# First block's input and first two weight pieces made one stage earlier, in the projection outputs' memory

## What is computed

```python
def rmsnorm(x, g):
    y = xf * lax.rsqrt(jnp.mean(xf * xf, axis=-1, keepdims=True) + NORM_EPS)
    return (y * g.astype(jnp.float32)).astype(x.dtype)

def swiglu(x, w_in, w_out):
    gate, up = jnp.split(x @ w_in, 2, axis=-1)
    return (jax.nn.silu(gate) * up) @ w_out

def decoder_layer(x, ...):
    x = x + 0.5 * swiglu(rmsnorm(x, lp['norm_ffn1']), lp['ffn1_w_in'], lp['ffn1_w_out'])
    h = rmsnorm(x, lp['norm_mix'])
    proj = h @ lp['w_in']
    ...
    x = x + jnp.concatenate([y_rwkv, y_sc, y_ssm], axis=-1) @ lp['w_out']
    x = x + 0.5 * swiglu(rmsnorm(x, lp['norm_ffn2']), lp['ffn2_w_in'], lp['ffn2_w_out'])
```

## Time and profile before

| | |
|---|---|
| median of 3 runs | 1755.36 us |
| the profiled execution's own time | 1752.43 us |
| its span in the profile | 1750.6 us |
| TensorE matmul busy | 1592.8 us, 91% of the span |
| VectorE / ScalarE / GpSimd busy | 58% / 48% / 35% |
| granted TensorE clock, mean | 0.966 |
| DMA | 256 MB, 146 GB/s over the span |

### The profile page before, as it was taken

The page is one execution under the profiler, slowest core; times in us unless marked ns, Lnnn a source line. Parts: engine busy times, 40 slices in busy tenths (PEclk is TensorE's granted clock), DMA queues, the critical chain, the costliest instruction groups (busy, mean ns, idle before and its releaser), DMA issues. The chain is left out here.

```text
span 1750.6 us, 41466 instructions
## 1 busy us (share of the span) xinstructions
PE 1592.8 (91%) x17389; PEld 1507.6 (86%) x17389; DVE 1010.7 (58%) x1704; ACT 843.0 (48%) x1480; POOL 618.0 (35%) x407
## 2 busy tenths in 40 slices
PE   5999999988789899999789999997987999899996
PEld 4999999886678789999789999997766888899995
DVE  3543377685689776343354434968667887554433
ACT  2545464656244555444344444665553445554431
POOL 0434412322075533434233343132204653334340
PEclk9999999989899999999999999999989999999997
DMA  5555557452054544555354555645403454455550
GB/s 171 172 167 184 158 157 207 149 152 72 3 143 130 148 148 158 185 193 175 114 161 162 193 175 167 194 148 174 124 1 85 127 175 116 142 174 187 178 166 25
DMA packets 280490, 256.28 MB, mean 146 GB/s; under 512 B 48022, under 2 KB 268540, under 8 KB 280290
## 3 DMA queue, kind: packets, MB, share of 16 engines
q1 hardware_dynamic: 276538, 252.05, 46.2%
q10 hardware_dynamic: 3768, 1.59, 0.4%
HBM read 242.22 MB, written 11.38 MB: 145 GB/s over the span
## 5 line engine op out<-in xcount | busy, mean ns | idle before, releaser
L223 PE MATMUL ps<-front_h_hi,front_hi 128*128 128x264 f32 x1520 | 451.4, 297 | 35.4 <-DVE front_lo L210 31.4
L210 POOL TENSOR_TENSOR front_lo<-front_raw,front_hi 128x1024 fp32r<-128x1024 f32 (+1 forms) x104 | 256.8, 2469 | 546.3 <-ACT front_hi L203 546.3
L224 PE MATMUL ps<-front_h_lo,front_hi 128*128 128x264 f32 x1520 | 439.3, 289 | 0.0
L225 PE MATMUL ps<-front_h_hi,front_lo 128*128 128x264 f32 x1520 | 438.8, 289 | 0.0
L203 ACT ACTIVATE front_hi<-front_raw 128x1024 fp32r<-128x1024 f32 (+2 forms) x238 | 246.7, 1039 | 287.5 <-PE ps L225 250.1
L223 PEld LDWEIGHTS ps<-front_h_hi,front_hi 128*128 128x128 f32 x1520 | 294.5, 194 | 43.5 <-issue 39.4
L210 POOL TENSOR_TENSOR out_lo<-out_raw,out_hi 128x1024 fp32r<-128x1024 f32 (+1 forms) x84 | 198.7, 2367 | 312.0 <-ACT out_hi L203 312.0
L224 PEld LDWEIGHTS ps<-front_h_lo,front_hi 128*128 128x128 f32 x1520 | 294.5, 194 | 1.3
L225 PEld LDWEIGHTS ps<-front_h_hi,front_lo 128*128 128x128 f32 x1520 | 292.6, 193 | 0.1
L203 ACT ACTIVATE out_hi<-out_raw 128x1024 fp32r<-128x1024 f32 (+1 forms) x168 | 173.2, 1038 | 222.1 <-PE ps L225 182.2
L210 DVE TENSOR_TENSOR front_lo<-front_raw,front_hi 128x1024 fp32r<-128x1024 f32 (+1 forms) x134 | 163.0, 1217 | 119.2 <-ACT front_hi L203 119.2
(11 more groups left out here) (375 smaller groups left out, 3373.2 us busy)
## 6 DMA issues: line engine op xcount, KB each, us to landing
front_raw<-in_w_in SPq DMA_DIRECT2D x50, 1024.0 KB, 5.2
front_raw<-in_ffn_w_in SPq DMA_DIRECT2D x44, 1024.0 KB, 6.0
out_raw<-in_ffn_w_in SPq DMA_DIRECT2D x44, 1024.0 KB, 5.4
back_sample_rows<-row_scratch SPq DMA_DIRECT2D x160, 128.0 KB, 3.0
out_raw<-in_w_out SPq DMA_DIRECT2D x16, 1024.0 KB, 5.2
front_raw<-in_ffn_w_out SPq DMA_DIRECT2D x16, 896.0 KB, 4.6
out_raw<-in_ffn_w_out SPq DMA_DIRECT2D x16, 896.0 KB, 4.6
front_raw<-in_ffn_w_out SPq DMA_DIRECT2D x8, 1024.0 KB, 4.9
```

Of the source, the lines that this page charges most:

```text
L210: eng.tensor_tensor(self.lo[n % self.RING][:, 0:k, 0:w], self._raw(n), self.hi[n % self.RING][:, 0:k, 0:w].bitcast(F32), ALU.subtract).the ...
L223: pe.matmul(out, hi[:, j, 0:w], x_hi[:, j], start=start and j == 0, stop=False)
L224: pe.matmul(out, hi[:, j, 0:w], x_lo[:, j], start=False, stop=False)
L225: mm = pe.matmul(out, lo[:, j, 0:w], x_hi[:, j], start=False, stop=stop and j == k - 1)
```

## The change

- `load_stage` also loads pieces 0 and 1 of layer 0's ffn1 (2 MB, behind the five other loads on SyncE's queue) and SyncE waits for them before the stage ends; the gains are copied out before x instead of after it; ScalarE and VectorE make h hi and h lo of layer 0, VectorE two tiles behind its copies.
- `back_stage` of layer 0 does the same for layer 1: the two loads stand behind all its own pieces, and h hi and h lo are made as `following` of ffn2. Layer 1's back stage has nothing following.
- `front_stage` no longer makes h, no longer waits for it (`h_made=True`) and reads pieces 0 and 1 where they lie (`resident`). Its three raw buffers begin with pieces 2, 3 and 4. `split_lo(1)` stands before the fold, and the mean behind product 1 instead of product 2.
- `xs` and `ys` are allocated once for the program; h hi, h lo and the two pieces lie over them.

```diff
 class Stream:
@@ load
-        if p >= self.raw_ring:
+        if p >= self.raw_ring + len(self.resident):
             n = max(self.last[q] for q in range(p - self.raw_ring + 1)) + 1
             sp.wait_ge(self.hi_ready, n)
...
@@ split_hi
-        act.wait_ge(self.loaded[p % self.raw_ring], self.landed[p])
+        if p >= len(self.resident):
+            act.wait_ge(self.loaded[(p - len(self.resident)) % self.raw_ring], self.landed[p])
...
+class NextInput:
+    def act_hi(self, act, k):
+        act.wait_ge(self.x_ready, k + 1)
+        act.activation(self.env.in_hi[:, k], self.env.x[:, k], ACT.Copy, scale=self.gain(k)).then_inc(self.hi_done, 1)
+
+    def dve_lo(self, dve, k):
+        dve.wait_ge(self.hi_done, k + 1)
+        dve.scalar_tensor_tensor(out=self.env.in_lo[:, k], in0=self.env.x[:, k], scalar=self.gain(k), in1=self.env.in_hi[:, k].bitcast(F32),
+                                 op0=ALU.mult, op1=ALU.subtract).then_inc(self.lo_done, 1)
+
+    def sp_weights(self, sp, w_in):
+        wi = w_in[self.layer].rearrange("(k p) c -> p k c", p=P)
+        for part in range(2):
+            sp.dma_start(self.env.first_raw[part][:], wi[:, :, part * FF:part * FF + 2 * P]).then_inc(self.weights_in, 16)
+        sp.wait_ge(self.weights_in, 32)
...
@@ load_stage
+                first.sp_weights(sp, d["ffn1_w_in"])
...
                 for k in range(KT):
+                    if k == KT - 1:
+                        pe.wait_ge(gains_copied, 1)
...
+            @block.scalar
+            def _(act):
+                act.wait_ge(gains_copied, 1)
+                for k in range(KT):
+                    first.act_hi(act, k)
+
             @block.vector
             def _(dve):
-                for k in range(KT):
-                    dve.wait_ge(turned, k + 1)
-                    dve.tensor_copy(env.x[:, k], env.ps[:, k, 0:N]).then_inc(copied, 1)
                 dve.wait_ge(gains_turned, 1)
-                dve.tensor_copy(env.gains[:], env.ps[:, KT - 1, N:N + (DEPTH + 1) * KT]).then_inc(copied, 1)
+                dve.tensor_copy(env.gains[:], env.ps[:, KT - 1, N:N + (DEPTH + 1) * KT]).then_inc(gains_copied, 1)
+                for k in range(KT + 2):
+                    if k < KT:
+                        dve.wait_ge(turned, k + 1)
+                        dve.tensor_copy(env.x[:, k], env.ps[:, k, 0:N]).then_inc(copied, 1)
+                    if k >= 2:
...
+                        first.dve_lo(dve, k - 2)
@@ front_stage
-        ffn = Ffn(st, env, "ffn1", ws, 0, norm1, at, None, following=norm2, side=vec, mean_after=2)
+        ffn = Ffn(st, env, "ffn1", ws, 0, norm1, at, None, following=norm2, side=vec, mean_after=1, h_made=True)
...
-                for p in range(3):
+                for p in range(2, 5):
                     ws.load(sp, p)
                 vec.sp(sp)
                 more = Part(side(sp))
-                for p in range(3, len(pieces)):
+                for p in range(5, len(pieces)):
...
-                for k1 in range(KT):
-                    norm1.act_hi(act, k1)
                 ws.split_hi(act, 0)
...
-                for k1 in range(KT):
-                    norm1.dve_lo(dve, k1)
                 ws.split_lo(dve, 0)
+                ws.split_lo(dve, 1)
                 norm1.dve_fold(dve)
-                ws.split_lo(dve, 1)
                 ws.split_lo(dve, 3)
@@ back_stage
-        ffn = Ffn(st, env, "ffn2", ws, OUT_HALVES, norm3, over, out_bank_free)
+        norm4 = NextInput(st, env, layer + 1) if layer + 1 < DEPTH else None
+        ffn = Ffn(st, env, "ffn2", ws, OUT_HALVES, norm3, over, out_bank_free, following=norm4)
+        if norm4 is not None:
+            norm4.x_ready = ffn.x_added
...
                 for p in range(3, len(pieces)):
                     ws.load(sp, p)
+                if norm4 is not None:
+                    sp.wait_ge(ws.used, OUT_HALVES)
+                    norm4.sp_weights(sp, d["ffn1_w_in"])
                 sp.wait_ge(s("stored"), 16 * RT)
```

More of the change, by code:

```diff
@@ L160, with __init__ @@
     RING = 4
-    def __init__(self, st, kp, pieces, halves, raw_ring=4, on_dve=None, buffers=None):
-        self.pieces, self.halves, self.raw_ring = pieces, halves, raw_ring
+    def __init__(self, st, kp, pieces, halves, raw_ring=4, on_dve=None, buffers=None, resident=()):
+        self.pieces, self.halves, self.raw_ring, self.resident = pieces, halves, raw_ring, resident
         if buffers is None:
@@ L188, in load @@
                     sp.wait_ge(self.lo_ready[eng], self.on_dve[:n].count(eng))
+        slot = (p - len(self.resident)) % self.raw_ring
         for (k, c0, w), src in self.pieces[p]:
-            sp.dma_start(self.raw[p % self.raw_ring][:, 0:k, c0:c0 + w], src).then_inc(self.loaded[p % self.raw_ring], 16)
+            sp.dma_start(self.raw[slot][:, 0:k, c0:c0 + w], src).then_inc(self.loaded[slot], 16)
     def _raw(self, n):
         p, c0, w, k = self.halves[n]
-        return self.raw[p % self.raw_ring][:, 0:k, c0:c0 + w]
+        if p < len(self.resident):
+            return self.resident[p][:, 0:k, c0:c0 + w]
+        return self.raw[(p - len(self.resident)) % self.raw_ring][:, 0:k, c0:c0 + w]
     def split_hi(self, act, n):
@@ L290, in pe_ready, with __init__, gain @@
         return ready
+class NextInput:
+    def __init__(self, st, env, layer, x_ready=None):
+        self.env, self.layer, self.x_ready = env, layer, x_ready
+        self.hi_done, self.lo_done, self.weights_in = st.sem("next_h_hi_done"), st.sem("next_h_lo_done"), st.sem("next_weights_in")
+    def gain(self, k):
+        return self.env.gains[:, self.layer * KT + k:self.layer * KT + k + 1]
+    def act_hi(self, act, k):
[10 more added lines that the diff above has]
+        sp.wait_ge(self.weights_in, 32)
 FFN_PARTS = ((0, 8), (8, 7), (15, 7))
@@ L318, with __init__ @@
 class Ffn:
-    def __init__(self, st, env, tag, ws, base, norm, place, bank_free, following=None, side=None, mean_after=1):
+    def __init__(self, st, env, tag, ws, base, norm, place, bank_free, following=None, side=None, mean_after=1, h_made=False):
         self.env, self.ws, self.base, self.norm, self.bank_free = env, ws, base, norm, bank_free
-        self.following, self.side, self.mean_after = following, side, mean_after
+        self.following, self.side, self.mean_after, self.h_made = following, side, mean_after, h_made
         at = 0
@@ L435, in pe @@
                 self.bank_free(pe, n)
-            ws.product(pe, base + n, env.ps[:, n % 4, 0:N], norm.h_hi, norm.h_lo, ready=norm.pe_ready(pe) if n == 0 else None)
+            ws.product(pe, base + n, env.ps[:, n % 4, 0:N], norm.h_hi, norm.h_lo, ready=norm.pe_ready(pe) if n == 0 and not self.h_made else None)
             if n == self.mean_after:
@@ L544, in load_stage @@
         gains_in, gains_turned = st.sem("gains_in"), st.sem("gains_turned")
-        eps_set, copied = st.sem("eps_set"), st.sem("x_copied")
+        eps_set, copied, gains_copied = st.sem("eps_set"), st.sem("x_copied"), st.sem("gains_copied")
+        first = NextInput(st, env, 0, x_ready=copied)
         with nc.Block() as block:
@@ L743, in front_stage @@
         rs = st.sb("norm_rs", [P, N])
-        norm1 = Norm(st, env, "ffn1", lambda k: env.gains[:, layer * KT + k:layer * KT + k + 1], EB, h_hi, h_lo,
+        norm1 = Norm(st, env, "ffn1", lambda k: env.gains[:, layer * KT + k:layer * KT + k + 1], EB, env.in_hi, env.in_lo,
                      at("ffn1_rs", 75904, [P, N]), at("ffn1_squares", 23232, [P, KT, N]), at("ffn1_root", 31680, [P, N]))
```

21 lines of the change are left out of this document (14 added, 7 removed).

## The result

The changed kernel takes 1728.96 us (median of 4 runs, 1721.52 to 1730.27) where the kernel before takes 1755.34 (4 runs, 1752.45 to 1758.56): a ratio of 0.9841, 95% interval 0.9808 to 0.9873. The forecast was 1731, the range 1724 to 1738.

A forecast was written before the change was run, and what follows sets the result against it. The prediction took TensorE to bound the first block once product 4 begins, so starting product 4 earlier moves everything after. Gains of 12.4 (layer 0) and 11.8 us (layer 1), 24.2 off 1755.4, gave 1731 us, range 1724 to 1738.

The forecast's parts named there:

- Layer 0's start: Layer 0's front stage begins at 17.82 instead of 16.73, product 0 at 20.24 instead of 24.40: 4.16 us earlier.
- Waits removed: TensorE's waits before products 1 and 4 of the front stages go: 5.08 us in layer 0, 6.01 in layer 1.
- The clock: One slow start at 1.2 GHz per layer instead of two, costing 2.0 us: 3.2 saved in layer 0, 0.8 in layer 1.
- Layer 1's start: Layer 1's front stage begins at 869.1 instead of 868.0, product 0 at 871.5: 4.95 us earlier.
- Sum: Product 4 comes 12.4 us earlier in layer 0 and 11.8 more in layer 1: 24.2 us, median 1731.
- Loads hidden: In layer 0's load stage the two new pieces land near 14.7, 2.5 us before VectorE ends, delaying nothing.
- Rival B: In layer 0's load stage the pieces share DMA engines; transposes start up to 6.0 us later: 1737 us, chance 0.05.
- Rival C: Piece loads, not TensorE, pace the first block; products from 5 on keep their old times: 1757.5 us, chance 0.04.
- Rival D: Lo tiles added to layer 0's back stage stall behind GpSimd splits, three pairs costing 7.1 us: 1738 us, chance 0.07.
- Rival E: Clock falls elsewhere make it slower; 60 us more low clock gives 1761 us; sign: longer time between layer starts; chance 0.03.

The follow-up runs named there:

- kernel 1: The changed kernel with the old order in the front stage (split lo 1 behind the fold, mean behind product 2): 1739.29 us, ratio 0.9927 to the kernel before.
- 2: The kernel before with the new order alone (split lo 1 ahead of the fold, mean behind product 1): 1733.31 us, ratio 0.9902 to the kernel before.
- Experiment 6: The changed kernel with extra transposes and matmuls into unused PSUM keeping TensorE at work over the stage change: 1725.24 us, ratio 0.9835 to the kernel before.
- 4: The changed kernel without the early loads (h made early, pieces 0 to 2 loaded in the front stage): 1737.44 us, ratio 0.9922 to the kernel before.
- kernel 9: The changed kernel with one added wait, GpSimd beginning split lo 2 only after VectorE's fold: 1727.02 us, ratio 0.9834 to the kernel before.
- kernel 10: The changed kernel with half 0 split in two steps, extra TensorE work, and split lo 2 behind the fold: 1727.85 us, ratio 0.9848 to the kernel before.

## Why the prediction was right

The time (1731 against 1728.96), the sign and the mechanism held, and by its steps:

- **Layer 0's start.** Product 0 at 20.57, 3.83 earlier; 4.16 was forecast. The front stage began 0.26 later than computed: the gains landed 0.14 later (8.86 against 8.72), the last copy of x began at 15.81 instead of 15.59, and the three lo tiles behind it ended at 17.44 instead of 17.2. The table load, which I had not costed, came only when the first copy of x was made (10.50), so h hi began late; it caught up by tile 3.
- **Waits removed.** Forecast 5.08 and 6.01: all gone. Experiments 1 and 2 show from both sides that the order does this: with the old order they return (1.63 and 2.06 before product 1, 1.16 before product 4); the new order alone removes them, for a wait of 0.45 before layer 0's mean.
- **The clock.** Forecast one slow start per layer at a cost of 2.0, bounds 1.25 and 2.8. Between product 0 and product 4, four products and the mean take 12.1 us at full clock by the earlier trace rows; the stretches took 13.47 and 14.27, so the slow starts cost 1.4 and 2.2. In the kernel before, the same reckoning gives 22.57 - 5.08 - 12.1 = 5.4 and 21.42 - 6.01 - 12.1 = 3.3, where I had booked 5.2 and 2.8. Savings: 4.0 and 1.1, forecast 3.2 and 0.8. The two later traces of the changed kernel give costs of 1.8 and 1.9 in layer 0 and 2.0 twice in layer 1, so the forecast of 2.0 held and 1.4 was a short one. Experiment 6 shows in layer 1 that the idle time is what costs it.
- **Layer 1's start.** Forecast 4.95; measured from the last update of x it is 4.90 (866.88 to 876.47 is 9.59, 853.83 to 858.52 is 4.69).
- **Sum.** Forecast 12.4 + 11.8 = 24.2 to product 4; measured 12.93 + 12.05 (and 0.12 in between). In layer 0 two misses cancel in part, 0.33 too much at product 0 and 0.8 too little for the clock. Over three traces the two starts give 25.0, 24.5 and 24.2. The medians fell by more: 26.4 us here, 28.5 and 28.3 on the other two chips. The 2 to 4 us beyond the sum lie outside the two starts; since the kernel before has one trace, no run shows whether they are the change's or scatter, and that the medians met 1731 within 2 us is in part luck.
- **Loads hidden.** Rival B: the gains landed at 8.86, before 8.72. Over all traces TensorE's first transpose of the gains starts at 8.42 to 8.72 in the three kernels without the two pieces behind them (before, 2, 4), mean 8.61, and at 8.85 to 9.54 in the ten with them, mean 9.11: the pieces cost about 0.5 us, not 0.14, and far less than rival B's 6.0. The Trainium skill, "DMA: Bandwidth & Descriptors", section "Two DMAs through the same engine are not ordered", lets a later descriptor finish its write before an earlier one; no trace here shows more than about 1 us of such lateness.
- **Rival C.** TensorE had no idle time to product 4, and from there to the last update of x took as long as before (819.8): not paced by loads, which would have kept the later products at their old times.
- **Rival D.** The three pairs of lo tiles in layer 0's back stage took 0.89 each, where ffn1's had taken 3.07; GpSimd had no split in hand at that moment. No TensorE wait followed.
- **Rival E.** After layer 1's product 4 three traces of one program differ by 6 us, some 4 of them in the pace of the same matmuls, and the stretch ahead of layer 1's start, whose growth the prediction had named as the sign of E, grew by 4 us in the third. Falls of the clock elsewhere do move the time, by a few us; the rival needed some 30 us.

What the prediction did not say is how its 24 us split between causes. It added them line by line, and that hid that the two moved lines, which need none of the memory or the new class, give 17 us alone, and the early work without them 13, of 27 to 28 for both. The parts overlap, so no share of the whole belongs to one of them.

## What to carry to other kernels

A split, or any step that an engine must do before the next product, should not stand in its engine's order behind a reduction that a later product needs: two moved lines alone gave 17 us here, against 27 to 28 for the whole change, and were the cheapest part to make. When two things cover each other at a stage's start (a load, and work beside it), price each alone and both together from the rows: moving one gains only up to where the other stands. Here product 0 came earlier by 0.3 us in layer 0 and 2.9 in layer 1 with the pieces alone, not at all with h alone, and by 3.5 and 5.0 with both. Price each removed idle stretch of TensorE with the slow stretch behind it: here another 1 to 4 us per layer besides the waits themselves.

## What the runs showed of the hardware

- With VectorE's fold and GpSimd's split side by side the fold takes 4.55 us, alone 2.47; where GpSimd's split begins 0.17 us behind a split on VectorE, GpSimd takes 3.29 instead of 2.40 to 2.52 and VectorE its usual 1.22. The Trainium skill, "SBUF — State Buffer", section "Who interferes with whom", says that a VectorE instruction with two SBUF inputs contends with a GpSimd instruction that reads SBUF; kernel 9 agrees, with the fold's 2.47 against 4.55.
- At the starts of the front stages TensorE's granted clock fell behind idle stretches of 2.06 us (kernel 1, layer 1) and 2.26 us (kernel 10), and held over 1.63 us in kernel 1 and over 1.50 and then 1.00 us, with work between, in kernel 6. Elsewhere it needs no long wait: in the kernel before it fell behind 2.30 us at 667.66 and, at 94.27, behind 4.27 us in which TensorE was never idle. So what a wait costs in clock can't be read off its length.

```profile
90.00:94.27 4.27, 4.27 (x66) 3.99 (x64) 1.14 (x3) 1.37 (x2) 2.30 (x1) 1.00 0.07 20
94.27:97.68 3.41, 3.41 (x17) 3.41 (x17) 0.00 (x0) 0.00 (x0) 0.05 (x1) 0.50 0.64 204
667.66 0.51 PE L223 MATMUL ps<-y_hi,out_hi 128*128 128x264 f32 x1 [2.30 <-DVE out_lo L210]
667.70:671.10 3.40, 3.40 (x16) 3.40 (x17) 3.40 (x3) 0.00 (x0) 2.04 (x1) 0.50 0.69 220
```

- The granted clock in the profile reads 1.00 in the first stretches of the span while the matmuls come at half pace (13 in 2.98 us): at the start of a trace the pace is the surer sign.
